# Splitting the start of an fp32-by-parts layer by tokens, and seven-product pairs in its last projection

## The reference, cut to what matters

```python
h = rms_norm(x, g_norm) * (1 + scale) + shift     # shift, scale, gate = silu(c) @ w_ada + b_ada
proj = h @ w_in                                   # 1024 -> 7168 columns
y_a = conv_branch(proj[:3072])                    # glu, 31 taps, layer norm, silu gate, @ w_a_out
y_b = pool_branch(proj[3072:5120])                # causal means, grouped product, silu gate, @ w_b_out
m = sigmoid(proj[5120:6144]) * y_a + sigmoid(proj[6144:]) * y_b
x = x + gate * (m @ w_out)
y = rms_norm(x, g_final)
```

## Time and profile before

| | us |
|---|---|
| median of 3 runs (lowest, highest) | 933.47 (932.53, 934.17) |
| the profiled execution's own time | 934.1 |
| its span in the trace | 932.3 |
| PE busy | 914.5 |
| DVE busy | 735.9 |
| ACT busy | 385.3 |

### The profile page before, as it was taken

The page is one execution under the profiler, slowest core; times in us unless marked ns, Lnnn a source line. Parts: engine busy times, 40 slices in busy tenths (PEclk is TensorE's granted clock), DMA queues, the critical chain, the costliest instruction groups (busy, mean ns, idle before and its releaser), DMA issues.

```text
span 932.3 us, 16713 instructions
## 1 busy us (share of the span) xinstructions
PE 914.5 (98%) x6928; PEld 896.3 (96%) x6928; DVE 735.9 (79%) x862; ACT 385.3 (41%) x540; POOL 88.5 (9%) x97
## 2 busy tenths in 40 slices
PE   7999999999999999999999999999999999999996
PEld 5699999999999999999999999999989999999996
DVE  1797999997999996999995999999897642443346
ACT  5583354434453443454433354435525321113242
POOL 0022221111021011111011210000000000000000
PEclk9999999999999999999999999999999999999998
DMA  9869989889688989799897984458851623152105
GB/s 368 341 159 231 251 214 259 225 254 241 162 224 251 256 235 266 171 243 260 242 269 235 235 194 141 140 171 287 355 227 49 250 102 146 46 189 85 46 1 182
DMA packets 77885, 191.20 MB, mean 205 GB/s; under 512 B 11633, under 2 KB 18289, under 8 KB 73841
## 3 DMA queue, kind: packets, MB, share of 16 engines
q1 hardware_dynamic: 48320, 119.61, 37.2%
q0 software_dynamic: 19328, 46.17, 24.7%
q10 hardware_dynamic: 10160, 24.35, 7.4%
HBM read 164.14 MB, written 80.49 MB: 262 GB/s over the span
## 4 chain that ended last, share of the span: by engine, by line
PE 80%; DVE 13%; DMA 4%; issue 1%; ACT 0%; SPq 0%; DVEq 0%; ACTq 0%
PE ps L918 16%; PE ps L912 16%; PE ps L914 16%; PE ps L849 10%; PE ps L852 10%; PE ps L850 10%; DVE conv_y L1641 5%; DMA ada_raw<-w_ada 2%; DVE hr L1520 1%; DMA raw<-w_sums 1%; DMA bf<-y_conv 1%; DVE stage_hi L1720 1%; DVE gr L1660 1%; PE ps L779 1%; PE ps L785 1%
## 5 line engine op out<-in xcount | busy, mean ns | idle before, releaser
L1641 DVE SCALAR_TENSOR_TENSOR conv_y<-conv_u,par_all,conv_y 128x1024 f32<-128x1024 f32 x240 | 300.4, 1277 | 2.1 <-DVE conv_y L1627 0.6
L914 PE MATMUL ps<-tr,hr 128*128 128x258 f32 x824 | 216.4, 283 | 0.0
L912 PE MATMUL ps<-tr,hr 128*128 128x258 f32 x824 | 215.5, 283 | 0.3 <-ACT u L1281 0.3
L918 PE MATMUL ps<-tr,hr 128*128 128x258 f32 x824 | 166.3, 283 | 0.0
L1215 ACT ACTIVATE hr<-raw 128x512 fp32r<-128x512 f32 (+1 forms) x188 | 115.7, 618 | 116.2 <-PE ps L918 87.4
L912 PE MATMUL ps<-hr 128*128 128x258 f32 x616 | 160.9, 282 | 1.3 <-DVE pool_u L1545 1.0
L914 PE MATMUL ps<-hr 128*128 128x258 f32 x616 | 161.5, 283 | 0.0
L912 PEld LDWEIGHTS ps<-tr,hr 128*128 128x128 f32 x824 | 156.9, 190 | 0.5 <-issue 0.5
L914 PEld LDWEIGHTS ps<-tr,hr 128*128 128x128 f32 x824 | 155.7, 189 | 0.0
L1520 DVE TENSOR_TENSOR hr<-raw,hr 128x512 fp32r<-128x512 f32 (+1 forms) x188 | 125.6, 672 | 5.3 <-ACT hr L1215 1.4
L918 PEld LDWEIGHTS ps<-tr,hr 128*128 128x128 f32 x824 | 127.2, 188 | 0.0
(11 more groups left out here) (200 smaller groups left out, 1272.4 us busy)
## 6 DMA issues: line engine op xcount, KB each, us to landing
w_sums<-w_main POOLq DMA_DIRECT2D x56, 512.0 KB, 9.3
raw<-w_sums SPq DMA_DIRECT2D x104, 256.0 KB, 4.6
raw<-w_main SPq DMA_DIRECT2D x82, 256.0 KB, 4.9
w_sums<-w_sums POOLq DMA_DIRECT2D x26, 512.0 KB, 5.5
w_raw<-w_main SPq DMA_DIRECT2D x24, 512.0 KB, 4.9
w_sums<-w_main ACTq DMA_DIRECT2D x22, 512.0 KB, 5.3
ada_raw<-w_ada SPq DMA_DIRECT2D x8, 1024.0 KB, 21.0
bf<-x_t SPq DMA_DIRECT2D x4, 1032.0 KB, 8.1
```

What stands on the lines that cost most here:

```text
L912: nc.tensor.matmul(bank[:, c, :], wh[:, w_cols], x_hi[:, k, t_cols], start=start and k == 0, stop=False, skip_group_check=True)
L914: nc.tensor.matmul(bank[:, c, :], wh[:, w_cols], x_lo[:, k, t_cols], start=False, stop=False, skip_group_check=True)
L918: last = nc.tensor.matmul(bank[:, c, :], wl[:, w_cols], x_hi[:, k, t_cols], start=False, stop=(k == n_k - 1), skip_group_check=True)
L1641: ins = v.scalar_tensor_tensor(out=y, in0=conv_u[:, x, k:k + SEQ], scalar=par_all[:, g, x, k:k + 1], in1=y, op0=ALU.mult, op1=ALU.add)
```

## The change: what it does

1. **Start by token parts.** Part 0 is chunks 0 and 1 (688 columns), part 1 chunk 2 (344, of them 336 prompt). For tiles 0 to 3 everything is done per part; tiles 4 to 7 stay whole. x comes in four DMAs of part 0 and, behind modulation block 1, two of part 1; the first weight halves move behind block 0, the second behind part 1. The silu of `c` moves ahead of the squares. The square sums, root, reciprocal and spread are done for each part, the second set in the middle of the first products.
2. **Output projection.** Tiles 2, 3 and 4, 5 of JOB_OUT become two pairs of the seven-product scheme (14 items), with four new block sums of m on DVE (2 x 516 x 4 columns), their hi parts on ACT and lo parts on DVE; their weight sums are a 14th chunk in DRAM. Tiles 0, 1 stay jobs, tiles 7, 6 go last. The residual x is loaded tile by tile.
3. **Taps' table.** Slot 0 costs 1470 ns in the planner (before 0), for the first value tiles.
4. **Smaller.** `var_sums` stands behind steps 5 and 7 (before 3 and 5); the mean rows 4 and 5 are added earlier in POOL's list.

```diff
+PART_CHUNKS = [(0, 1), (2,)]
+PART = [slice(0, 2 * CW), slice(2 * CW, TOK)]
+PART_PROMPT = [slice(0, 2 * CW), slice(2 * CW, SEQ)]
+QCOLS = [2 * CW // QUADS, CW // QUADS]
+H_STEPS = [(0, 0), (1, 0), (2, 0), (3, 0), (0, 1), (1, 1), (2, 1), (3, 1), (4, None), (5, None), (6, None), (7, None)]
+H_COUNT = {step: n + 1 for n, step in enumerate(H_STEPS)}
+OUT_A, OUT_B = N, N + 1
+OUT_TILE = {OUT_A: 2, OUT_B: 4}
+OUT_ITEMS = [("P1", OUT_A), ("P1", OUT_B), ("P6", OUT_A), ("P2", OUT_A), ("P7", OUT_A), ("P5", OUT_A), ("P4", OUT_A), ("P3", OUT_A),
+             ("P6", OUT_B), ("P2", OUT_B), ("P7", OUT_B), ("P5", OUT_B), ("P4", OUT_B), ("P3", OUT_B)]
...
-COST = {"lo": 580, "half": 680, "tap": 1165, "first_tap": 1900, "last_tap": 2270, "level": 1130, "out": 2100, "pool_lo": 1150, "mix": 1370}
+COST = {"first_value": 1470, "lo": 580, "half": 680, "tap": 1165, "first_tap": 1900, "last_tap": 2270, "level": 1130, "out": 2100, "pool_lo": 1150, "mix": 1370}
...
-    form, n = ITEMS[slot - 1] if slot else ("", 0)
+    if slot == 0:
+        return COST["first_value"]
+    form, n = ITEMS[slot - 1]
...
-        sp.dma_start(bf[:, 2 * n:2 * n + 2, :], t["x_t"][:, 2 * n:2 * n + 2, :]).then_inc(x_loaded[n], 16)
-    for s in range(2):
-        sp.dma_start(w_raw[:, s, 0:FORM_COLS], t["w_main"][s][:, 0:FORM_COLS]).then_inc(first_half_loaded[s], 16)
+        rows = slice(2 * n, 2 * n + 2)
+        sp.dma_start(bf[:, rows, PART[0]], t["x_t"][:, rows, PART[0]]).then_inc(x_loaded[n], 16)
     for q in range(4):
         for half in range(2):
             k = slice(half * KT // 2, (half + 1) * KT // 2)
             sp.dma_start(ada_raw[:, q, k, :], t["w_ada"][q][:, k, :]).then_inc(ada_loaded[q][half], 16)
         if q == 0:
+            for s in range(2):
+                sp.dma_start(w_raw[:, s, 0:FORM_COLS], t["w_main"][s][:, 0:FORM_COLS]).then_inc(first_half_loaded[s], 16)
+        if q == 1:
+            for n in range(2):
+                rows = slice(n * KH, (n + 1) * KH)
+                sp.dma_start(bf[:, rows, PART[1]], t["x_t"][:, rows, PART[1]]).then_inc(x_rest_loaded[n], 16)
             for s in range(2):
                 sp.dma_start(w_raw[:, s, FORM_COLS:], t["w_main"][s][:, FORM_COLS:]).then_inc(raw_full[s], 16)
...
-        if k == 3:
+        if k == 5:
...
-        if k == 5:
+        if k == 7:
...
+    act.wait_ge(c_loaded, 16)
+    act.wait_ge(c_padded, 1)
+    nc.scalar.activation(c_act[:, :, 0:NMOD], c_in[:], ACT.Silu).then_inc(c_ready, 1)
     nc.scalar.activation(eps[:, 2:3], eps[:, 0:1], ACT.Sqrt)
...
+    single(JOB_OUT + 1, m_hi, m_lo)
...
+    for i, (form, n) in enumerate(OUT_ITEMS):
+        pe.wait_ge(item_lo, OUT_SPLIT + i + 1)
+        if form == "P1":
+            pe.wait_ge(dve_evac, FIRST_STRASSEN - 1 + (n - OUT_A) - JOB_B)
+            block_product(OUT_SPLIT + i, bank_a(n), gr[:, 0:KH, HALVES[0]], gr[:, KT:KT + KH, HALVES[0]], start=True).then_inc(item_done, 1)
...
+    out_t_hi("P5", 1)
+    out_t_hi("P7", 2)
+    item_split(OUT_SPLIT)
+    item_split(OUT_SPLIT + 1)
+    out_t_hi("P6", 3)
+    out_t_hi("P4", 4)
+    tile_square(0, 0)
+    item_split(OUT_SPLIT + 2)
+    item_split(OUT_SPLIT + 3)
+    out_seed(OUT_A)
+    tile_square(1, 1)
...
+    ot1, ot2, ot3, ot4 = (out_t(form, 1, full=True) for form in ("P5", "P6", "P7", "P4"))
+    m_rows = hf[:, KT:2 * KT, :]
+    link(v.tensor_tensor(ot1, m_rows[:, 0:KH, HALVES[0]], m_rows[:, 0:KH, HALVES[1]], ALU.subtract))
+    dve.sem_inc(t_summed, 1)
+    link(v.tensor_tensor(ot3, m_rows[:, KH:KT, HALVES[1]], m_rows[:, 0:KH, HALVES[1]], ALU.subtract))
+    dve.sem_inc(t_summed, 1)
+    dve.wait_ge(gate_ready, 2)
+    v.tensor_scalar(minus_gate[:], mod[:, 4:6, :, 0], -1.0, None, ALU.mult)
+    plain_x(0)
+    item_lo_part(OUT_SPLIT)
+    item_lo_part(OUT_SPLIT + 1)
+    link(v.scalar_tensor_tensor(out=ot2, in0=ot1, scalar=-1.0, in1=m_rows[:, KH:KT, HALVES[1]], op0=ALU.mult, op1=ALU.subtract))
+    dve.sem_inc(t_summed, 1)
+    link(v.scalar_tensor_tensor(out=ot4, in0=ot2, scalar=-1.0, in1=m_rows[:, KH:KT, HALVES[0]], op0=ALU.mult, op1=ALU.subtract))
+    dve.sem_inc(t_summed, 1)
+    out_t_lo("P6", 3)
+    plain_x(1)
+    item_lo_part(OUT_SPLIT + 2)
+    item_lo_part(OUT_SPLIT + 3)
+    out_t_lo("P7", 2)
+    out_t_lo("P5", 1)
+    add_square(1)
+    for i in range(len(OUT_ITEMS)):
+        out_result(i)
+        if i + 4 < len(OUT_ITEMS):
+            item_lo_part(OUT_SPLIT + i + 4)
+        if i == 0:
+            out_t_lo("P4", 4)
```

More of the change, by code:

```diff
@@ new lines, in _ @@
+            load_x(0)
+            load_x(1)
+            for i in range(4):
+                load_out_item(i)
+            sp.wait_ge(x_new_ready, 1)
+            load_x(2)
+            sp.wait_ge(x_new_ready, 2)
+            load_x(3)
+            for i in range(4, len(OUT_ITEMS)):
+                load_out_item(i)
+            sp.wait_ge(x_new_ready, 3)
+            load_x(5)
+            sp.wait_ge(x_new_ready, 4)
+            load_x(4)
+            sp.wait_ge(item_lo, OUT_SPLIT + 12)
+            sp.dma_start(w_raw[:, 1, :], t["w_main"][MAIN_B + JOBS - 1 - JOB_B]).then_inc(raw_full[1], 16)
@@ L762, in _ @@
             pool.wait_ge(ada_loaded[3][1], 16)
-            for step in range(3 * (N // 2) + 3):
+            for step in range(3 * SUM_CHUNKS + 3):
                 c, k = step // 3, step % 3
@@ L770, in _ @@
                     add_row(MEAN_AT[step])
-            for r in range(4, 6):
-                add_row(r)
         @block.tensor
@@ L836, in _ @@
                 pe.wait_ge(x_squared, e + 1)
[L837 removed]
+                last = square_sums(0, e)
                 if e < KT - 1:
@@ L866, in _, with first_steps @@
             together = KT - 3
-            def first_steps(k, jobs=(0, 1)):
+            def first_steps(k, part=None, jobs=(0, 1)):
                 if k == 0:
@@ L1380, in final_square, with tile_square, out_t_hi @@
                 nc.scalar.activation(row, row, ACT.Copy, scale=vecs[:, G_FINAL, m:m + 1]).then_inc(x_new_scaled, 1)
-            for m in range(KT - 2):
-                split_for(JOB_OUT + m)
-                final_square(m, m, 0, TOK)
+            def tile_square(n, m):
+                if n >= 2:
+                    act.wait_ge(x_new_added, n - 1)
+                final_square(n, m, 0, TOK, sq_tile if n else sq_sum)
+            def out_t_hi(form, count):
+                act.wait_ge(t_summed, 4 + count)
+                nc.scalar.activation(out_t(form, 0), out_t(form, 1, full=True), ACT.Copy).then_inc(t_hi_done, 1)
@@ new lines, in out_seed, with last_hi @@
+            def out_seed(n):
+                act.wait_ge(item_done, LAST + OUT_AT["P1", n] + 1)
+                if n == OUT_A:
+                    act.wait_ge(dve_evac, FIRST_STRASSEN - JOB_B)
+                else:
+                    act.wait_ge(c11_out, n)
+                nc.scalar.activation(bank_b, bank_a(n), ACT.Copy).then_inc(seeded, 1)
+            def last_hi(slot, n, items):
+                act.wait_ge(item_done, LAST + items)
+                act.wait_ge(raw_full[slot], raw_count(FIRST_STRASSEN + slot))
+                nc.scalar.activation(w_hi[:, slot, n], w_raw[:, slot, n], ACT.Copy).then_inc(w_hi_done, 1)
@@ L1462, in _ @@
-            dve.wait_ge(rstd_copied, 2)
-            for q in range(4):
+                dve.wait_ge(h_hi_done, H_COUNT[e, part])
+                v.scalar_tensor_tensor(out=hr[:, KT + e, columns], in0=bf[:, e, columns], scalar=mod[:, q, j, 0:1],
+                                       in1=hr[:, e, columns].bitcast(F32), op0=ALU.add, op1=ALU.subtract).then_inc(h_lo_done, 1)
+            dve.wait_ge(rstd_copied, 1)
+            modulation(0)
+            h_tile(0, 0)
+            first_split(0, 0)
```

413 lines of the change are left out of this document (275 added, 138 removed).

## The result

| | before | after |
|---|---|---|
| median, us | 933.96 (932.26 to 936.36, 7 runs) | 936.46 (934.60 to 938.92, 7 runs) |
| ratio, 95% interval | | 1.0031 (1.0016 to 1.0047) |
| profiled execution: time / span | 934.1 / 932.3 | 934.6 / 932.8 |

So 2.5 us slower, 0.27%: a little beyond the 0.2% that I took as the bound of what can be told. The profiled execution of after is the fastest of its seven, 0.5 us above the profiled one of before. So what follows accounts for those 0.5 us first; why the other six are slower is a question of its own.

A forecast was written before the change was run, and what follows sets the result against it. PE was taken as the bound, busy for 914.5 of 932.3 us. The terms: 934.1 + 7.0 (start) - 5.1 (projection) - 1.2 (table) - 0.5 (variance sums) = 934.3, at the median 933.7; range 928.5 to 938.0.

The forecast's parts named there:

- The sum for an execution like the profiled one: Whole kernel: 934.1 + 7.0 - 5.1 - 1.2 - 0.5 = 934.3 us, before the step to the median.
- The start's chain: Start, link by link over the engines: first step at 25.8 us, last full copy at 64.5, job 2's weights at 68.1.
- The start's term: Start up to job 2: job 2 starts 7.4 us later, 6.6 with shorter sums; taken as +7.0 us.
- The projection: Output projection: four jobs of 45.44 us become 14 items of 40.37, -5.1 us, if DVE and ACT keep up.
- The table: Taps' planner table: PE waits of 1.0 and 0.3 us go; -1.2 us, bounds -1.3 and 0.
- The variance sums: `var_sums` two steps later: 1.7 us wait covered, a later split keeps the gain to -0.5 us, bounds -1.7 and +0.5.
- The tail: End of the kernel: keeps its order, so nothing gained or lost.
- The step that failed: From profiled execution to median: the profiled one stood 0.6 us above the median, so 934.3 became 933.7.
- rival (d): PE's clock in the start's new gaps: at the lower level some products take 3 us more, 936.5 us; chance 0.08.
- Rival (a): Start stays dense, between -1.5 and +3 us: time 925.2 to 929.7, intermediate cases to 931.6; chance 0.24.
- Rival (b): Start costs more, +9 to +10 us, through part 1's sums or late x: 936 to 938 us; chance 0.18.
- Rival (c): New wait at the output projection's first items, half its gain lost: 936 us; chance 0.08.

The follow-up runs named there:

- e: Changed kernel with modulation block 1's second half and its turn moved ahead of the first product on TensorE: 932.91 us.
- f: Changed kernel with the full copies of tiles 2 and 3 ahead of hi parts 6 and 7 on ScalarE: 935.01 us.
- h: Changed kernel with both order edits, those of e and f, together: 930.44 us.
- i: h with the second part's norm left out, the third chunk scaled with the first chunk's reciprocal roots: 927.07 us.
- b: Kernel before with the new start alone (loads, norm and products in two parts, modulation block 0 early): 942.96 us.
- g: Changed kernel with 31 matmuls without use filling four gaps of TensorE in the first steps: 937.13 us.
- a_rest: Changed kernel with its start put back as before (loads, norm, first steps, engine orders): 926.14 us.

## Why the prediction was right, and where it was off

The forecast was 933.7 (range 928.5 to 938.0) with 0.42 for no change and 0.34 for slower; the result, 936.46, lies inside the range, 2.8 above the likeliest time, and by 0.2% just on the slower side.

**The sum for an execution like the profiled one** was 934.3; it took 934.6. Its steps:

- *The start's chain* held link by link, its times within 1 us. Squares from 7.85 (7.67 forecast), reciprocal 15.59 to 16.82 (end at 16.5), first product 26.65 (25.8), VectorE idle 4.4 before the second `mod` (4.1), gaps of TensorE of 2.6, 1.1, 1.4, 1.2 and 2.0 (3.1, 0, 1.3, 1.3, 2.2), last copy at 64.8 (64.5), job 2's split at 68.24 (68.1), job 2 at 68.29 (68.2). I missed the gap of 1.1 before the first part's step 2. My prices by width were low for narrow pieces: a tile of 688 and of 336 columns took VectorE 0.94 and 0.57 us where I had 0.88 and 0.46, and ScalarE's hi part 0.87 and 0.58 where I had 0.8 and 0.43.
- *The start's term* was +7.0 and measured +7.8. I had 7.4 by the chain and took it down with a second case of short sums. The sums of part 1 were indeed shorter than my 0.3 to 0.4 us, eight in 1.39 us (my floor of 0.05 an instruction stood on no row; it came to 0.022), and this changed nothing: at that point TensorE is ahead of VectorE. The other 0.4 is job 2's start of before, which I put at 60.8 and which is 91.31 - 68.29 = 23.0 us ahead of the last result, 60.5.
- *Which waits carry it*: I named two, VectorE's for turn 1 and the six copies. Experiments e, f and h show 6.0 us for them. I treated the second norm's chain as a gap of 1.3 of TensorE; it is worth 3.4 to 3.8 (i).
- *The projection*, -5.1: -5.0 in the profile, -5.3 alone. No wait stands among the items.
- *The table*, -1.2 with bounds -1.3 and 0: -1.9, whose interval of -0.6 to -2.6 holds the forecast. The planner's table, worked through again, has two taps fewer only until slot 31 and one fewer until 39, not two until 39; the sum doesn't hang on it. *The variance sums*, -0.5: -0.8 by the profile, -1.5 by the medians, and the split that I named is what waits, for 0.9. Together -1.8 in after's profile, against -1.7.
- *The tail*, nothing: -0.5. Without it the sum would have been 0.8 short, the start's error, and not 0.3; that much of the match is luck.

**The step that failed** is the last one: "that stood 0.6 above the median, so 933.7". I carried the distance between profiled execution and median over from before. In after the profiled execution stands 1.9 below the median. The likeliest reason is that the new start makes stretches at the lower clock more frequent, and that by chance this execution's was hidden; the 1.6 us between after's and b's first jobs is what such a stretch costs where it isn't. It is not shown for after's own executions: two of them took 936.0 and 936.3 us at a mean clock of 0.996, above the profiled one's 0.995, and without a trace nobody can say where their stretch was, or if they had one. It is rival (d), to which I gave 0.08: stretches were there, and at 936.5 it had the time nearly right. The gap that (d) names, before the first product, is where a stretch of b, f and g falls (and one of i, which hasn't this gap); in after's profiled execution it came behind the 2.0 us gap before step 6.

The rule of the Trainium skill that I set beside rival (d) ("TensorE: Matmul & The Clock Gate", HAM oscillation: idle waits between bursts bring the half clock back) agrees with after's row at 60 to 63 us, though the waits of the Trainium skill's own example are longer, about 3 to 5 us, and the gap here was 1.98. But a_rest is at half clock where its only gap is a wait of 1.34 us for block 1's second half, and before has the same wait there (1.43) at full clock. a_rest first, then before:

```profile
28.00:31.00 3.00, 3.00 (x14) 1.34 (x15) 3.00 (x5) 2.55 (x5) 0.00 (x0) 0.50 1.02 423
```

```profile
28.00:31.00 3.00, 2.55 (x19) 1.55 (x14) 3.00 (x4) 2.55 (x5) 0.00 (x0) 1.00 1.00 418
```

So a gap is not enough to tell whether it comes.

By the medians two larger errors stand against each other. The start costs 8.9 us (b) to 10.5 (after against a) and not 7.0, and the parts without it give -8.0 and not -6.8. Forecast and result are 2.3 apart (+0.2 and +2.5) because the second makes up for a part of the first; that the result lies inside the range owes something to this.

The other rule of the Trainium skill, of 1.38 us of drain behind a table load ("ScalarE: Activation LUTs", What ACT_TABLE_LOAD costs), is not borne out here either: after's load for the silu runs from 4.86 for 1.28 us, and the silu starts at 6.16.

```profile
4.86 1.28 ACT L1281 ACT_TABLE_LOAD   x1 [4.86 <-DMA c_in<-c_t]
6.16 0.27 ACT L1281 ACTIVATE c_act<-c_in 128x72 f32<-128x72 f32 x1
```

Rival (a), a dense start, fell: the first product did come 3.8 us earlier and none of it was left. Rival (b) had the time (936 to 938), and its +9 to +10 for the start is what the medians give, but for the wrong reason: neither the sums nor the third chunk's load was late. Rival (c) fell, no item waited.
